# Moving the gate projection of one tile out of the expert loop of the tile before it

## What is computed

```python
branches = jnp.stack([o_a, o_b, o_c, o_d], axis=2)       # four attention-like branches, 256 wide each
proj  = jnp.einsum('bsnc,ncd->bsnd', branches, w_branch)
gates = jax.nn.sigmoid(m_g)                              # m_g: 4096 of the columns of x @ w_in
mix   = jnp.sum(gates * proj, axis=2) @ w_out
x = _layer_norm(DN_ALPHA * x + mix, ln1_g, ln1_b)
x = _layer_norm(DN_ALPHA * x + peer_ffn(x, peer_wq, peer_keys, peer_u, peer_v), ln2_g, ln2_b)

def peer_ffn(x, ...):                                    # 8 heads, the 16 best of 16384 experts each
    s = einsum(x @ wq, sub_keys); expert, gate = two rounds of top 16
    act = gelu(einsum('btd,bthkd->bthk', x, u_tab[expert]))
    return einsum('bthk,bthkd->btd', gate * act, v_tab[expert])
```

## Time and profile before

| | |
|---|---|
| median of 3 runs | 2890.86 us (2890.68 to 2893.79) |
| profiled execution: its own time | 2890.68 us |
| profiled execution: span in the trace | 2888.9 us |
| first expert gather, last expert gather | 1146.7 us, 2862.2 us |
| mean granted TensorE clock | 0.879 of full |
| DMA bytes over the span | 839.34 MB, mean 291 GB/s |

### The profile page before, as it was taken

One profiled execution on the slowest core, in us unless ns is written; L12 is line 12 of the kernel. 1 busy time (PEld: TensorE's weight loads), 2 busy tenths in 40 slices (PEclk: granted clock), 3 DMA queues, 4 the chain that ended last, 5 costly groups with the idle time before them and its releaser, 6 DMA issues.

```text
span 2888.9 us, 34008 instructions
## 1 busy us (share of the span) xinstructions
PE 2348.2 (81%) x13488; PEld 1987.6 (69%) x13488; DVE 1392.3 (48%) x3171; ACT 1304.9 (45%) x2335; POOL 744.4 (26%) x615
## 2 busy tenths in 40 slices
PE   7987998969999999878786878787688777666675
PEld 6766887856884887867565867666687665565554
DVE  3564333341001234664656664545755544686444
ACT  1551112210000230576656566754556774556665
POOL 0010102110000001234434323333423323334663
PEclk9988999989999999988887898899797989676666
DMA  6221111123432767999999999999998999999997
GB/s 260 88 90 59 59 59 66 52 75 143 146 146 109 271 228 293 420 420 368 406 365 416 404 421 369 399 415 417 400 420 343 415 369 421 396 381 357 421 419 317
DMA packets 109999, 839.34 MB, mean 291 GB/s; under 512 B 12176, under 2 KB 12432, under 8 KB 13968
## 3 DMA queue, kind: packets, MB, share of 16 engines
q0 software_dynamic: 73728, 536.90, 45.7%
q1 hardware_dynamic: 36112, 300.25, 26.5%
HBM read 836.06 MB, written 1.05 MB: 290 GB/s over the span
## 4 chain that ended last, share of the span: by engine, by line
PE 49%; DMA 20%; DVE 15%; ACT 11%; issue 3%; POOL 2%; SPq 0%; DVEq 0%; POOLq 0%; ACTq 0%
DMA mem<-in_puv,mem 20%; PE psm L431 10%; PE psm L2144 7%; PE psm L439 5%; PE psm L1714 4%; DVE mem L2188 4%; ACT mem L2162 3%; PE psm L718 3%; PE psm L2019 3%; PE psm L1247 3%; PE psm L1350 2%; PE psm L1906 2%; PE psm L1398 1%; PE psm L733 1%; ACT L2157 1%
## 5 line engine op out<-in xcount | busy, mean ns | idle before, releaser
L2144 PE MATMUL psm<-mem 128*128 128x128 f32 x4096 | 685.7, 324 | 365.2 <-ACT mem L2162 364.6
L2172 POOL DMA_INDIRECT mem<-in_puv,mem x512 | 623.3, 1217 | 1076.4 <-PE psm L2144 1011.1
L2144 PEld LDWEIGHTS psm<-mem 128*128 128x128 f32 x4096 | 573.0, 168 | 473.6 <-ACT mem L2162 455.3
L2188 DVE CUSTOM_DVE_ANT_0 mem<-mem 128x1024 f32<-128x1024 f32 x512 | 625.6, 1227 | 458.3 <-DMA mem<-in_puv,mem 457.4
L2162 ACT ACTIVATE mem<-mem 128x1024 f32<-128x1024 f32 x512 | 588.8, 1150 | 16.7
L431 PE MATMUL psm<-mem 128*128 128x256 f32 (+2 forms) x1504 | 352.3, 398 | 32.8 <-DVE mem L1180 16.6
L431 PEld LDWEIGHTS psm<-mem 128*128 128x128 f32 x1504 | 293.3, 198 | 91.1 <-issue 30.2
L2157 ACT ACTIVATE mem<-mem 128x1 f32<-128x1 f32 x512 | 101.9, 199 | 462.6 <-DVE mem L2188 461.7
L1714 PE MATMUL psm<-mem 128*128 128x256 f32 x1024 | 252.3, 398 | 0.5 <-ACT mem L1426 0.5
L1714 PEld LDWEIGHTS psm<-mem 128*128 128x128 f32 x1024 | 198.9, 202 | 27.8 <-ACT mem L1426 0.9
L439 PEld LDWEIGHTS psm<-mem 128*128 128x128 f32 x1408 | 179.6, 193 | 45.3 <-issue 22.0
(11 more groups left out here) (357 smaller groups left out, 2422.9 us busy)
## 6 DMA issues: line engine op xcount, KB each, us to landing
mem<-in_w2g SPq DMA_DIRECT2D x64, 1024.0 KB, 9.0
mem<-in_w SPq DMA_DIRECT2D x18, 2048.0 KB, 8.3
mem<-in_pwq SPq DMA_DIRECT2D x32, 1024.0 KB, 10.0
mem<-in_w2f SPq DMA_DIRECT2D x28, 1024.0 KB, 9.8
mem<-in_wgu SPq DMA_DIRECT2D x11, 2048.0 KB, 8.0
mem<-in_w2t SPq DMA_DIRECT2D x20, 1024.0 KB, 10.6
mem<-in_w2b SPq DMA_DIRECT2D x16, 1024.0 KB, 10.8
mem<-in_w2o SPq DMA_DIRECT2D x16, 1024.0 KB, 10.4
```

The costliest lines, as they stand in the source:

```text
L2144: m = pe.matmul(bank(6 + c // 4)[:, tsl(c % 4)], GR[n % PING][:, 1024 + c * 128:1152 + c * 128], ident, is_transpose=True, start=k == 0 an ...
L2172: po.indirect_dma_start(GR[n % PING], None, A[f"puv{i // 2}"], bass.IndirectOffsetOnAxis(ap=IX[i % 2][:, k:k + 1], axis=0)).then_inc(gsem[ ...
L2188: ve.tensor_tensor_reduce(out=GR[n % PING][:, 0:1024], in0=GR[n % PING][:, 0:1024], in1=X[:, i % 2, :], scale=1.0, scalar=0.0, op0=MUL, op ...
```

## The change

The division of tile 1's gates ends: all 32 steps go ahead of the experts of tile 0, 12 beside the last 8 mix steps (before: 4) and 20 beside the 20 routing steps (before: 12). None is left in the lane. Tile 1's gates then use banks 4 and 5 throughout, the wait for banks 0 and 1 falls away, and `core` of tile 1, which takes bank 4, waits for the last group of gates instead of group 3. The order of the weight loads follows the plan.

```diff
@@ tile_steps, plan
-            attend = weave([("gates", 16 if i == 1 else 32, 1), ("nsa", 22, 1), ("core", 14, 0.7)])
+            attend = weave([("gates", 32 * (i != 1), 1), ("nsa", 22, 1), ("core", 14, 0.7)])
...
-        plan += [(s, int(s == "gates")) for s in weave([("mix", 8, 0.5), ("gates", 4, 1)]) + ["query"] * 8
-                 + weave([("route", 20, 1), ("gates", 12, 1)])]
+        plan += [(s, int(s == "gates")) for s in weave([("mix", 8, 0.5), ("gates", 12, 1)]) + ["query"] * 8
+                 + weave([("route", 20, 1), ("gates", 20, 1)])]
@@ core_pe
             if i == 1:
-                pe.wait_ge(*GTA[1, 3])
+                pe.wait_ge(*GTA[1, 7])
@@ gates_bank
-            return bank(4 * (i == 1 and j < 4) + j % 2)
+            return bank(4 * (i == 1) + j % 2)
@@ gates_pe
                 pe.wait_ge(*landed2("g", i, n))
-                if i == 1 and n == 8:
-                    pe.wait_ge(*MA[i, ("t", 5)])
                 if n % 2 == 0 and n >= 4:
```

## The result

The changed kernel takes 2912.67 us (median of 4 runs, 2907.26 to 2915.78) against 2892.07 us before: +20.6 us, ratio 1.0068 with a 95% interval of 1.0051 to 1.0087. The forecast was 2895 within 2885 to 2904. The profiled execution has a span of 2917.1 us and took 2918.9 us, 6 us over the median of the others, so its stretches and gathers show the loss somewhat large.

The account below looks back on a forecast made before the run. The prediction took DMA bytes to bound tile 0's expert stage, and TensorE with a chain of waits the stretch ahead. Terms: +14.0 - 10.0 = +4.0 us on 2890.7, so 2895 us, range 2885 to 2904.

Parts of the forecast that it names:

- Part 1: Beside tile 0's last mix steps: 8 more gates steps delay transposes, query, scores, sorting and first gather by 14.0 us.
- Part 2: Beside routing: 160 gate records instead of 96, ending about 1179.5 us; TensorE 28 us late, first expert about 1186.
- Part 3: Tile 0's expert stage: four loads, 4.2 MB, fewer for the DMA engines after the first gather, -10.0 us.
- Part 4: From first to seventh gather, 27 us: 14.4 MB on offer for 11.3, so DMA stays full, 0 us of idle.
- Part 5: Waits: the dropped wait for banks 0 and 1 and core's wait for all gates groups cost 0 us.
- A: Rival: DMA runs dry before the seventh gather as last weight loads land late; 4 to 8 us, 2899 to 2903; chance 0.20.
- B: Rival: TensorE's clock drops to 1.2 GHz in the longer gate products, up to 6.8 us, 2902; chance 0.10.
- C: Rival: DMA holes at 1320 and 1450 us close; one 2889, chance 0.12; both 2884.6, chance 0.08.
- D: Rival: freed TensorE time shortens the expert stage by more than the bytes, at most -14 us, 2877; chance 0.05.

Follow-up runs that it names:

- e3: Changed kernel with only 4 gates steps beside mix and 28 beside and behind routing, none in the lane; 2908.68 us.
- e4: Kernel before without the 8 loads of tile 1's gate weights 8 to 15, their 64 products computed from a tile in memory; 2880.41 us.
- e7: Changed kernel with 8 gate loads and 64 products put back into the lane, into banks nobody reads; 2920.02 us.
- e2: Changed kernel with 16 lane steps of useless TensorE products from tiles in memory in the gates' old place, without their loads; 2910.63 us.
- e16: e4 with the compression burst of each tile cut into four steps of the plan; 2856.69 us.
- e0: Changed kernel unaltered, run and profiled again; 2910.04 us.
- e5: Kernel before with the 8 loads of tile 1's gate weights 8 to 15 kept but 56 of their 64 products left out; 2888.51 us.
- e9: Changed kernel with the compression products of tile 1 cut from 64 to 2; 2901.37 us.
- e14: Kernel before with the compression burst of each tile cut into four steps of the plan, experts between, same work and result; 2859.64 us.
- e8: Changed kernel with tanh in place of exp in tile 1's nsa stage, which saves ScalarE's table loads; 2903.65 us.
- e1: Changed kernel with 16 empty steps in the lane where the gates stood; 2917.68 us.
- e10: Kernel before with 4 more of tile 1's gates steps (2 loads) beside routing, 12 left in the lane; 2904.71 us.
- e13: Kernel before with the compression burst of each tile cut into two steps of the plan, experts between, same work and result; 2876.91 us.
- e12: Changed kernel with only 8 of the 64 products of gate loads 8 to 15, loads, waits and order kept; 2906.60 us.
- e11: Kernel before with 4 fewer of tile 1's gates steps beside routing, 20 in the lane; 2892.18 us.

## Why the prediction was wrong

**Part 1** (first gather 14 us later) was right in size: 96 records in 20.88 us, the gather 11.9 and 14.3 us later in two executions. As a term of the sum it doesn't stand by itself: e3 takes the 14 us away and gains 1.4, as loads take their place. (The 32 gate products end at 1119.9 by the earlier trace rows and not at 1119.75, which changes nothing.)

**Part 2** (gates end at 1179.5, first expert at 1186) was right for the products: 35.03 us, to 1177.5. The first expert came at 1190.6 by 6.2 us of waits for loads.

**Part 3 is the step that failed**: four loads, 10.0 us "less for the DMA engines after the first gather", each load at 2.5 us, its transfer time at 420 GB/s. The count held: gate loads 13 and 14 were issued between 1155 and 1158 us, ahead of the first gather, and 15 behind it. The price did not. The eight loads taken from this lane are worth 9.8 us (e4), 10.5 (e7 to e2) or 4 to 7 (e16), so 0.5 to 1.3 us each. The share of 0.98 in the earlier trace rows was read as "the bytes set the pace". The runs fit another reading: the bytes and the engines' own rounds took about the same time, and the ring filled what gaps there were with weights fetched ahead, so that with fewer bytes the GB/s fall and the time hardly does.

**Part 4** (no idle ahead) was right up to 1190 and then not: 276 GB/s instead of 420 from 1190 to 1200 us is 3.4 us of standstill (2.0 in e0, with 334 GB/s). The prediction's -10.0 us is +10.0 for four loads that still come behind the first gather, less 20.0 for the eight that leave the lane. Its 14.0 + 10.0 = 24 us late before the lane gives anything back is close, in spite of the standstill, to the changed kernel's 21 to 23 us at gather 32.

**Part 5** (the waits cost nothing) was not tried alone.

Put together: forecast +24 in front and -20 in the lane. By the account it was +30 (e7) and -11; by the changed kernel's own gathers and its medians +21 to +23, and between nothing and 4 back. Both ways most of the miss is the relief of the lane that didn't come. That the clock falls in the thinner lane (0.74 for 0.82 from 1400 to 1512 us) belongs to it, and the prediction gave it no term.

**The rivals.** A came in part, and was not the cause. TensorE was 4.6 us later than 1186 and the seventh gather went out at 1192.8, both as A says. But only 1.2 us of the waits were for the feature load that it named and none for gate 15; 5.0 us were for query loads. By its own test, a share under about 0.8 between 1180 and 1195 us, it fails: 0.92, and 1.01 in e0. The standstill was 2 to 3.4 us where it priced 4 to 8, and its 2899 to 2903 us are 10 to 14 short. B (clock in front) did not come: 1.00 from 1112 to 1160 us. C (holes close) went the other way: they grew. D has e5's and e2's answer: TensorE's freed time is worth 1.7 us or less than nothing. None of the rivals said that the loads might be worth half of their transfer; by the prediction's own sum that is +24 - 10 = +14 us, 2905, just above the range.

Of the two rules of the Trainium skill: the limit of about 358 GB/s for HBM per core ("DMA: Bandwidth & Descriptors", "Specifications") is not what this trace shows, with 420 over 140 us (1160 to 1300) before and 427 in 10 us after. That queues take turns (same page, "Queues, rings and completion order") agrees with loads issued between 1159 and 1178 that took 10.3 to 18.0 us to land in the changed kernel, again more than half rate explains.

**What stays open.** Which engine sets the lane's pace when the bytes are gone isn't settled. The burst (e9, e14) has a part, and table loads (e8) and TensorE's clock (e2 against e1) probably have. Not settled either is why e10 costs 11 to 14 us, what opens e7's hole at 1280 us, and how much of the small differences is the accident of which step falls beside which expert: e13 gains nothing in tile 1 (+3.8 at gather 128) and all of its time later. e12 and e3 show that loads and products ahead of the experts can't be added up separately.

The fastest version with the same result is e14, at 2859.64 us, 31 us under the kernel before. It leaves the gates where they were.

## What to carry to other kernels

A stage whose DMA is 0.98 busy is not yet a stage where a load is worth its transfer time: where the loads run ahead in a ring, take some out and look at the GB/s before counting on it. Work moved ahead of a pipeline that is waiting to start is free while it fits into the first wait of the engine that does it (9.00 us in e11, 2.08 before, the same time). What it costs beyond that has to be measured: e10 is 6.6 us late at the seventh gather, has made this up by gather 16, and loses 11 to 14 us behind it. And if a stage streams through a few buffers, look for the longest single step that stands between two buffer releases; cutting one of 128 short records in four brought more than anything that was moved, though part of it may have come by the clock.

## What was unexpected of the hardware

Sixty-four products that nobody reads made the kernel no slower and probably some 5 to 7 us faster (e2 against e1): TensorE's granted clock in that stretch was 0.85 instead of 0.72, between its levels of 2.4 and 1.2 GHz. The compression burst shows what a level is worth: 64 records took 7.00 us in the changed kernel, where the granted clock was 0.50, and 32 took 1.96 us in e14, where it was 1.00; that is 3.92 for 64.
